# Splitting a mixer's output projection in two and running one half between attention turns

## The reference, cut to what matters

```
x = rmsnorm(x)*g_first           (the end of the block before)
h = rmsnorm(x)*(1+sc1) + sh1
o_hg  = hgrn2_mixer(...)         # 4 recurrent heads of 128 columns: 512 columns
o_nsa = nsa_mixer(...)           # 8 heads of 64: gated sparse attention: 512 columns
x = x + g1 * (concat([o_hg, o_nsa], -1) @ w_out)     # 1024 x 1024
h = rmsnorm(x)*(1+sc2) + sh2
x = x + g2 * moe_ffn(h)          # router, 64 experts, shared expert
```

## Time and profile before

| what | value |
|---|---|
| median of 3 timed runs | 3318.27 us |
| profiled execution, span from first to last instruction | 3322.3 us |
| gated attention on PE (first score to last value) | 2381.6 to 2474.0 us |
| `out_2` on PE | 2474.0 to 2519.5 us |
| last L2240 of the stage ends | 2522.4 us |
| experts (`routed`) begin | about 2573 us |
| PE, DVE, ACT busy over the span | 98%, 58%, 52% |

### The profile page before, as it was taken

One profiled execution on the slowest core, in us unless ns is written; L12 is line 12 of the kernel. 1 busy time (PEld: TensorE's weight loads), 2 busy tenths in 40 slices (PEclk: granted clock), 3 DMA queues, 4 the chain that ended last, 5 costly groups with the idle time before them and its releaser, 6 DMA issues.

```text
span 3322.3 us, 48526 instructions
## 1 busy us (share of the span) xinstructions
PE 3247.3 (98%) x16468; PEld 2621.4 (79%) x16468; DVE 1924.6 (58%) x2441; ACT 1722.1 (52%) x2077; POOL 1340.7 (40%) x675
## 2 busy tenths in 40 slices
PE   8999999999999999999999999999989999999998
PEld 7888887678888788888778888778866788888784
DVE  4335683663345433461373333357667899999897
ACT  5552334545533555331445542522463788888884
POOL 3444442044444444444224444434302444444441
PEclk9999999999999999999999999999999999999999
DMA  3234331022244232443422223223103999999997
GB/s 128 95 100 163 122 104 58 8 95 95 95 145 152 82 99 97 136 155 111 130 83 95 99 94 99 100 76 105 58 11 121 359 378 385 387 389 385 370 368 303
DMA packets 128451, 534.41 MB, mean 161 GB/s; under 512 B 24432, under 2 KB 24688, under 8 KB 100464
## 3 DMA queue, kind: packets, MB, share of 16 engines
q1 hardware_dynamic: 107488, 499.63, 42.5%
q0 software_dynamic: 20736, 33.60, 2.7%
q10 hardware_dynamic: 144, 0.08, 0.0%
HBM read 531.64 MB, written 41.94 MB: 173 GB/s over the span
## 4 chain that ended last, share of the span: by engine, by line
issue 49%; PE 29%; POOL 15%; DMA 3%; DVE 3%; ACT 1%; POOLq 1%; SPq 0%; DVEq 0%; ACTq 0%
POOL w_lo L2105 15%; PE ps L883 8%; PE ps L885 7%; PE ps L884 7%; PE ps L1454 2%; DMA big<-in_exp_gu 1%; DMA big<-slot_rows 1%; PE ps L1547 1%; PE ps L1205 1%; PE ps L1243 1%; PE ps L1166 0%; PE ps L1158 0%; DVE hid L2866 0%; PE ps L1473 0%; PE ps L1349 0%
## 5 line engine op out<-in xcount | busy, mean ns | idle before, releaser
L2105 POOL TENSOR_TENSOR w_lo<-stage_buf,w_hi 128x1024 fp32r<-128x1024 f32 (+1 forms) x396 | 969.6, 2449 | 1481.7 <-ACT w_hi L1635 1481.6
L1635 ACT ACTIVATE w_hi<-stage_buf 128x1024 fp32r<-128x1024 f32 (+1 forms) x396 | 414.7, 1047 | 1175.9 <-PE ps L885 1116.7
L883 PE MATMUL ps<-x_hi,w_hi 128*128 128x512 f32 x1984 | 773.3, 390 | 4.5 <-POOL w_lo L2105 2.8
L885 PE MATMUL ps<-x_hi,w_lo 128*128 128x512 f32 x1984 | 772.0, 389 | 0.0
L884 PE MATMUL ps<-x_lo,w_hi 128*128 128x512 f32 x1984 | 771.9, 389 | 0.0
L883 PE MATMUL ps<-hid,w_hi 128*128 128x512 f32 x1312 | 518.6, 395 | 4.5 <-issue 1.7
L885 PE MATMUL ps<-hid,w_lo 128*128 128x512 f32 x1312 | 511.6, 390 | 0.0
L884 PE MATMUL ps<-hid,w_hi 128*128 128x512 f32 x1312 | 510.8, 389 | 0.0
L883 PEld LDWEIGHTS ps<-x_hi,w_hi 128*128 128x128 f32 x1984 | 372.4, 188 | 86.4 <-POOL w_lo L2105 4.9
L884 PEld LDWEIGHTS ps<-x_lo,w_hi 128*128 128x128 f32 x1984 | 372.4, 188 | 77.1
L885 PEld LDWEIGHTS ps<-x_hi,w_lo 128*128 128x128 f32 x1984 | 372.4, 188 | 77.0
(11 more groups left out here) (403 smaller groups left out, 4808.3 us busy)
## 6 DMA issues: line engine op xcount, KB each, us to landing
stage_buf<-in_gu SPq DMA_DIRECT2D x176, 512.0 KB, 3.3
big<-in_exp_gu SPq DMA_DIRECT2D x72, 1024.0 KB
h_buf<-in_exp_gu SPq DMA_DIRECT2D x72, 1024.0 KB
s_buf<-in_exp_dn SPq DMA_DIRECT2D x72, 1024.0 KB
stage_buf<-in_down SPq DMA_DIRECT2D x64, 512.0 KB, 3.6
stage_buf<-in_down SPq DMA_DIRECT2D x32, 384.0 KB, 3.2
sil_buf<-in_ada SPq DMA_DIRECT2D x24, 512.0 KB, 4.1
tmp_buf<-in_ada SPq DMA_DIRECT2D x24, 512.0 KB, 4.2
```

The source lines that it names most:

```text
L883: nc.tensor.matmul(o, a_hi, b_hi, start=start, stop=False)
L885: return nc.tensor.matmul(o, a_lo, b_hi, start=False, stop=stop)
L1635: nc.scalar.activation(w_hi[s][:, 0:n], stage[s][:, 0:n], ACT.Copy).then_inc(upper_done, 1)
L2105: nc.gpsimd.tensor_tensor(w_lo[s][:, 0:n], stage[s][:, 0:n], w_hi[s][:, 0:n].bitcast(F32), ALU.subtract).then_inc(parted, 1)
```

## The change

The weights of `out_2` are laid out again on the host: unit j of the first four holds, for two output tiles, the four contraction tiles of the recurrent heads, and the last four units hold the attention's. On the chip:

- PE does the first half in 16 pieces, `first_half(i - 3)` at i = 3 to 18 of `gated`, each two contraction tiles by three matmuls. Two pieces make one output tile in bank 3.
- Scores now rotate over three banks. Three of a unit's four come first; the fourth comes inside the turning of unit i-2, behind its first or second piece. 
- `keep_clock` has 12 matmuls in place of 24. `spread_factor("first")` moves to i = 2, and DVE copies the factor out of bank 3 (`first_rows`), so that `first_norm` reads it from SBUF.
- DVE does the split of operand tiles 0 to 6, the eight `first_norm(k)` and the eight additions `add_half(m)` inside `gated`. ACT does operand tiles 0 to 6 and the upper parts of weight units 2, 3 and 4 there too, and GpSimd the rests of these units when ACT is done.
- After `gated`, `second_half` does the other contraction for 8 output tiles in banks 0 to 3, and `add_rest` adds, squares and sums tile after tile.

```diff
                 for i in range(len(units) + 3):
                     if i < len(units):
-                        for k, (b, n, q, kk) in enumerate(units[i]["mms"]):
-                            if i > 0:
-                                pe.wait_ge(att["sc_read"], 4 * i + k - 3)
-                            nc.tensor.matmul(ps[:, b, 0:n], q, kk, start=True, stop=True).then_inc(att["sc_ready"], 1)
+                        for k in range(3):
+                            score(i, k)
...
                     if i == 2:
                         pe.wait_ge(att["c_less"], 1)
                         head_rows(3)
+                        spread_factor("first")
+                    if i < 2:
+                        score(i, 3)
+                    if i >= HALF_AT:
+                        first_half(i - HALF_AT)
...
-                            keep_clock(4 + un["pieces"][0] % 2, 24)
+                            keep_clock(4 + un["pieces"][0] % 2, 12)
                         pe.wait_ge(att["probs"], j + 1)
                         for m, k in enumerate(un["pieces"]):
                             turn(k, [n_s[j % 3][:, a:a + P] for _, a, _ in un["chunks"][4 * m:4 * m + 4]])
+                            if i < len(units) and m == min(1, un["t"]):
+                                score(i, 3)
...
+                def score(i, k):
+                    _, n, q, kk = units[i]["mms"][k]
+                    if 4 * i + k >= 3:
+                        pe.wait_ge(att["sc_read"], 4 * i + k - 2)
+                    nc.tensor.matmul(ps[:, (4 * i + k) % 3, 0:n], q, kk, start=True, stop=True).then_inc(att["sc_ready"], 1)
...
+            def first_half(n):
+                m, at = n // 2, PART_AT["out_2"]
+                if n % 2 == 0:
+                    pe.wait_ge(half["read"], m + 1)
+                wh, wl = out_weights(m // 2)
+                for k in (2 * (n % 2), 2 * (n % 2) + 1):
+                    pe.wait_ge(x_ready, at + k + 1)
+                    c = 4 * (m % 2) + k
+                    last = three(ps[:, 3, :], wh[:, c, :], wl[:, c, :], out_hi[:, k, :], x_lo[:, k, :], k == 0, k == 3)
+                if n % 2 == 1:
+                    last.then_inc(units_done if m % 2 else half["ps"], 1)
...
+            def second_half():
+                at = PART_AT["out_2"]
+                pe.wait_ge(att["sc_read"], 4 * len(n_units))
+                for n in range(4):
+                    wh, wl = out_weights(4 + n)
+                    for ks in (range(4, 7), range(7, 8)) if n == 0 else (range(4, 8),):
+                        for m in (2 * n, 2 * n + 1):
+                            if m == 3:
+                                pe.wait_ge(half["read"], KD + 1)
+                            elif m >= 4:
+                                pe.wait_ge(h_ready, H_AT["mix_2"] - KD + m - 3)
...
                     gated()
-                    spread_factor("first")
-                    dense("out_2", "out_2")
+                    second_half()
```

In `gated` on ACT:

```diff
+                    if i in (1, 2):
+                        operand(i + 1, hg["o_out"], i + 2, hi=out_hi)
+                    if i in (7, 12, 16):
+                        upper("out_2", 0, 2, {7: 2, 12: 3, 16: 4}[i])
+                    if i in (9, 13, 17):
+                        p = (i - 9) // 4
+                        operand(4 + p, att["out"], p + 1, hi=out_hi)
```

In `gated` on DVE, the second part behind the scaling of unit i-1, and `add_rest` after it:

```diff
                     if i == 2:
                         hgrn_head_out(3)
+                        first_rows()
+                    if i >= HALF_AT + 1 and (i - HALF_AT) % 2 == 1 and i <= HALF_AT + 2 * KD:
+                        add_half((i - HALF_AT - 1) // 2)
...
+                    if i in (1, 2, 3):
+                        operand("out_2", x_hi=out_hi, ks={1: (0, 1), 2: (2,), 3: (3,)}[i])
+                    if i >= HALF_AT and (i - HALF_AT) % 2 == 0 and i < HALF_AT + 2 * KD:
+                        first_norm((i - HALF_AT) // 2)
+                    if i == 5:
+                        clear_squares()
+                    if i in (10, 14, 18):
+                        operand("out_2", x_hi=out_hi, ks=(4 + (i - 10) // 4,))
...
+            def add_rest():
+                for m in range(KD):
+                    out_tile(KD + m)
+                    dve.wait_ge(half["read"], m + 2)
+                    nc.vector.scalar_tensor_tensor(out=h[:, m, :], in0=ps[:, m % 4, :], scalar=mod[:, 16 + m:17 + m], in1=h[:, m, :],
+                                                   op0=ALU.mult, op1=ALU.add).then_inc(h_ready, 1)
+                    dve.wait_ge(h_ready, H_AT["mix_2"] - KD + m + 1)
+                    add_square(h[:, m, :])
```

More of the change, by code:

```diff
@@ L393, in block_kernel @@
                 turns_n += 2
+        half = {n: sem(f"half_{n}") for n in ("ps", "read")}
+        HALF_AT = 3
+        out_hi = tiles(hid_buf[:, 0:KD * T], T)
         es_ready = sem("es_ready")
@@ L1213, in gated, with out_weights @@
                         last.then_inc(att["pv"], 1)
+            def out_weights(n):
+                pe.wait_ge(parted, CUT["out_2"] + n + 1)
+                return (tiles(w[n % 2], P) for w in (w_hi, w_lo))
+            def first_half(n):
[20 more added lines that the diff above has]
+                                pe.wait_ge(h_ready, H_AT["mix_2"] - KD + m - 3)
+                            for k in ks:
+                                pe.wait_ge(x_ready, at + k + 1)
+                                c = 4 * (m % 2) + k - 4
+                                last = three(ps[:, m % 4, :], wh[:, c, :], wl[:, c, :], out_hi[:, k, :], x_lo[:, k, :], k == 4, k == 7)
+                            if k == 7:
+                                last.then_inc(units_done if m % 2 else half["ps"], 1)
             def hgrn():
@@ L1972, in _ @@
                     upper("out_2", 0, 2, 1)
+                    for k in range(2):
+                        operand(k, hg["o_out"], k + 1, hi=out_hi)
                     gated()
-                    for k in range(KD):
-                        operand(k, *((hg["o_out"], k + 1) if k < 4 else (att["out"], k - 3)))
-                    weights("out_2")
+                    upper("out_2", 0, 2, 5)
+                    operand(7, att["out"], 4, hi=out_hi)
+                    upper("out_2", 0, 2, 6)
+                    upper("out_2", 0, 2, 7)
                 elif st == "moe":
@@ L2291, in columns, with operand @@
                 dve.sem_inc(rcol_ready, 1)
-            def operand(name, shift=None):
-                for k in range(KD):
+            def operand(name, shift=None, ks=range(KD), x_hi=x_hi):
+                for k in ks:
                     dve.wait_ge(x_hi_ready, PART_AT[name] + k + 1)
@@ L3066, in _ @@
                     gated()
-                    operand("out_2")
-                    first_norm()
-                    residual("out_2", st, mod[:, 16:24])
+                    operand("out_2", x_hi=out_hi, ks=(7,))
+                    add_rest()
                 elif st == "moe":
```

31 lines of the change are left out of this document (23 added, 8 removed).

## The result

The changed kernel takes 3329.56 us (median of 6, 3328.33 to 3332.63), the kernel before 3318.26 (median of 6, 3316.55 to 3321.83) on the same chip. The ratio is 1.0031 with a 95% interval of 1.0021 to 1.0040: slower by 11.3 us, where 6.9 were forecast. The profiled execution of the changed kernel has a span of 3326.9 us and a time of 3328.78. Only 4.6 us of the 11.3 show in the spans, because its first score stands at 2375.90 and not at 2381.60: the part ahead of it, which the change hardly touches, ran faster in this execution. Summed over its windows, that part lost 3.4 us to the lower clock here and 8.5 us in the execution of the kernel before. The comparison must therefore start at the first score. From there to the first product of the router the changed kernel takes 159.8 us, the kernel before 148.3.

What follows compares the result with a forecast made beforehand. DVE was taken to bound the stretch before 2409.91, with PE's later gaps mostly waits for DVE's scaling. The terms summed to 147.7 us against 140.8, 6.9 more, hence 3325 us, with a range of 3312 to 3336.

Steps and rivals of the forecast that it cites:

- torn scores: Attention, units 6 to 15: third and fourth scores without partners cost 0.77 us more at 512 columns, 5.2 us together.
- To the turn of unit 3: From 2381.6 to the turn at 2409.91: 28.3 us as before plus 4.8 us of added DVE work, 33.1 us.
- the halves 0 to 2: Half pieces at i = 3 to 5: fit beside DVE's added work at nothing, otherwise 1.4 us each.
- From there to the last value: After unit 3's turn: 73.1 us of PE work with 13 half pieces, plus torn scores, kind changes, waits and locks.
- The waits of 2.0 us: Attention turns: PE waits for DVE's scaling, queued behind the late fourth mask, 2.0 us (bounds 0 and 8).
- The locks of 1.7: Attention turns: GpSimd's L2105 and DVE instructions exclude each other, upon a scaling at i = 12, 1.7 us.
- The second half: From the last value to the last L2240: DVE's 8 tiles of 2.47 us set the pace, 28.6 us.
- The clock behind it: Turning of `h`: PE idle some 5 us before it, then a lower clock costs 1.5 us (bounds 0 and 1.5).
- slower by DVE's queue: Rival, 13 turns: late fourth score holds up the scaling, 0.6 us more wait each, 8 us, 3333 us; chance 0.18.
- Even: Rival, attention: lone scores or locks cost half, turns run with fewer waits, 3320 us; chance 0.22.
- Faster: Rival: DVE's 4.8 us before 2409.91 hidden, clock stays up, no L2105 on two-input DVE instructions, 3313.6 us; chance 0.10.

Runs made afterwards that it cites:

- early split: Changed kernel with DVE's split of operand tile 3 moved from iteration 3 to iteration 2: 3331.92 us, ratio 1.0036 to the kernel before.
- pairs: Changed kernel with scores 0 and 1 in front and 2 and 3 together inside the turning, from unit 2 on: 3331.91 us, ratio 1.0034.
- tearing alone: Kernel before with only the fourth score of units 2 to 15 moved into the turning, in its old bank: 3333.16 us, ratio 1.0039.
- the kernel with parts of the halves left out: Changed kernel with 9 of 12 matmuls of each output tile's first half left out: 3296.96 us, not comparable; stretch to the last value 72.90 against 80.96 us.
- the best mends: Changed kernel with tile 3 split earlier, scores two and two, second half's squares on ACT, filler at units 1 to 3: 3324.16 us, ratio 1.0012.

## Why the prediction was right, and where its terms were off

The forecast was 3325 us with a range of 3312 to 3336, the most weight on same or slower; 3329.56 lies in it, 4.6 us above the forecast and so just outside the 4 us on either side that the forecast itself was given. The direction and the reason hold: DVE's added work ahead of the turn of unit 3, torn scores, and gaps smaller than the halves. That the sum comes as near as it does is in part luck: the first term is 6.1 us too small and that of the second half 2.8 too large. By its own terms, in the profiled execution:

- **To the turn of unit 3: 33.1 us, measured 39.2** (2375.90 to 2415.07). This is the term that was mis-sized, by 6.1 us. I counted the work that DVE gets (4.8 us) and let "the halves 0 to 2" fit beside it at nothing. I did not follow the order in which the two queues meet at i = 4: piece 1 ahead of the fourth score, the split behind the scaling. The ring is worth 2.3 us at full clock (early split), and most of the rest is clock, for which the sum had nothing new here: the first stretch lost 5.1 us to it (42.26 times 0.12) where 1.6 were lost before.
- **From there to the last value: 84.5 us, measured 84.0** (2415.07 to 2499.12). Of its parts, the torn scores were 5.2 us and measured 3.4 (pairs) to 4.6 (tearing alone). I took the upper end, and for a lone score even that was too low (two records at 0.43 are 0.87 us): a lone score of two records takes 1.06 us, and four records in pairs take 1.06 as well (2459.26 to 2460.32 with pairs). By these rows the tearing would be 6.75 times 1.05, 7.1 us. The kernel before with it alone shows that part of that hides in PE's waits (idle 6.7 us of its second stretch before, 4.6 then); and scores in pairs don't give all of it back, since two groups of four records take 2.12 us where eight together take 1.92. The Trainium skill (TensorEngine Tiling (Array Packing), "Key Properties") says that tiles run in parallel; this agrees. The waits of 2.0 us measure 1.5 (80.96 less 79.49 busy). The locks of 1.7 measure nothing at the end: one `first_norm` takes 2.87 us in place of 0.75, with 3.46 us to spare behind it, and the subtraction that I saw fall upon a scaling at i = 12 (2466.74) meets DVE as it waits for PE.
- **The second half: 28.6 us, measured 25.8** (2499.12 to 2524.89). A tile costs DVE 2.24 and not 2.47 us, since the square now follows the addition at once; and the stops by GpSimd are two of 1.3 us, where I had 3.6. The Trainium skill (SBUF — State Buffer, "Who interferes with whom") has a DVE instruction with two SBUF inputs and a GpSimd read exclude each other; the trace agrees, 1.99 us against 0.69, and 2.87 against 0.75 for the `first_norm` that reads its factor from SBUF.
- **The clock behind it: 1.5 us, measured 3.1** in this execution, nothing in the early split, the pairs and two more, and 1.7 in the kernel with parts of the halves left out (10.61 us at 0.84). PE's gap was 2.3 us, not 5.

Of the rivals, *slower by DVE's queue* was wrong as a pattern: PE waits in the second stretch for 1.5 us in all. It was right at one turn, the one at i = 4. *Even* had the torn scores at half their price; they cost 3.4 to 4.6 of 5.2 us. *Faster* asked for DVE's 4.8 us to be hidden and a clock that stays up; neither happened. With the best mends DVE's work still isn't hidden: their first stretch is 36.6 us at full clock (43.59 at 0.84) against 29.6. A mechanism that I priced too low is the clock. About 5 of the 11.3 us are more time at half the clock, mostly in the first stretch. The kernel before with the tearing alone has a lower clock over its runs: 0.9930 against 0.9957. At one place the trace shows an order of things: the clock is 1.00 from 2396 to 2399, PE then waits 3.34 us to 2402.80, and from 2402 on the clock is 0.50. That is an order in one execution and not a cause shown: in the execution of the same program up to there with 0.75, the half piece behind the same wait of 3.34 us still runs at its full pace, and most of the loss lies ahead of any half piece. The early split takes this wait away, and the clock fell ahead of it instead. Why it falls at other places in executions of one program, and what decides where, stays open.

## What to carry to other kernels

Before work is moved into an engine's idle time, read what the gaps wait for: here they waited for DVE, DVE got more to do, and of the moved matmuls' time 63% came out at the end. Follow the new order of both queues through the one turn where the added pieces first meet, instruction by instruction; a sum of busy times does not show a ring. Leave pairs of products that run side by side together: the torn fourth score alone cost about 4 us of work and some 9 that went with a lower clock, as much as the whole change. And take a change's clock from the mean of many runs, not from one profile: here the same first stretch took 42.26 us in one execution and 49.21 in another.

## What the runs showed of the hardware

- Two executions of the same instructions got a clock of 0.88 (42.26 us) and 0.75 (49.21 us) in the first stretch. Time by mean clock scatters less than the time within most sets of runs (2.4 us against 3.6 as standard deviations in the 35 of the kernel before, 1.7 against 3.1 in the 11, but 2.6 against 2.3 in the 15). Between these three sets it is no steadier: it moves by 1.2 us (3304.8 to 3306.0), the medians by 1.0 (3320.06 to 3321.02).
- A float32 score with 64 rows costs 1.06 us at 512 columns, alone or with its partner on the other half of the partitions.
- A DVE instruction on 128x512 with two inputs in SBUF takes 1.99 or 2.87 us instead of 0.69 or 0.75 where it runs beside GpSimd's subtraction. The additions with one input in PSUM (L2718) take 0.75 us beside it as well.
- Matmuls on zeros are not a sure means to hold the clock: 12 more at unit 2 left it at 0.76 in the first stretch, while four fillings in the kernel before went with 1.00 in place of 0.97 in its second stretch and a mean clock of the runs of 0.9964 against 0.9951.
